# Two heads' compressed scores per product, the first norms inside the compression, and the first causal parts in front of the meeting

## The reference, cut to what matters

```python
h = _rmsnorm(x, norm1_g); proj = h @ w_in
q = _rmsnorm(proj[..., :o1].reshape(B, T, N_KV, HPG, HEAD_DIM), q_norm_g)   # 16 heads of 64, 4 groups
kv = proj[..., o1:o2].reshape(B, T, 6, N_KV, HEAD_DIM)
k_cmp = _rmsnorm(_compress(kv[:, :, 0], ...), k_norm_g[0])   # 31 blocks of 32 tokens; einsum, gelu, einsum
v_cmp = _compress(kv[:, :, 1], ...)
k_slc = _rmsnorm(kv[:, :, 2], k_norm_g[1]); k_win = _rmsnorm(kv[:, :, 4], k_norm_g[2])
s = jnp.einsum('bqghd,bngd->bghqn', qb, k_cmp) * scale
p_cmp = _masked_softmax(s - slopes * dist, dist >= 0)
o_cmp = jnp.einsum('bghqn,bngd->bqghd', p_cmp, v_cmp)
o = gb[..., 0:1] * o_cmp + gb[..., 1:2] * o_slc + gb[..., 2:3] * o_win
```

## Time and profile before

| | us |
|---|---|
| median of three runs | 3345.44 |
| the profiled execution's own time | 3342.76 |
| its span | 3341.0 |
| PE busy | 3247.5 (97% of the span) |
| DVE busy | 1785.4 (53%) |
| ACT busy | 1297.1 (39%) |
| mean granted TensorE clock | 0.978 |

### The profile page before, as it was taken

One profiled execution on the slowest core, in us unless ns is written; L12 is line 12 of the kernel. 1 busy time (PEld: TensorE's weight loads), 2 busy tenths in 40 slices (PEclk: granted clock), 3 DMA queues, 4 the chain that ended last, 5 costly groups with the idle time before them and its releaser, 6 DMA issues.

```text
span 3341.0 us, 41312 instructions
## 1 busy us (share of the span) xinstructions
PE 3247.5 (97%) x15343; PEld 2620.3 (78%) x15343; DVE 1785.4 (53%) x2671; ACT 1297.1 (39%) x1849; POOL 205.7 (6%) x230
## 2 busy tenths in 40 slices
PE   8989998999999999999999999999999999999998
PEld 6668976888888888876688888888888668888887
DVE  7357696445553455335765555345553566555532
ACT  4227755233332333323266333333322325633332
POOL 1001100000000000010110000010000011010000
PEclk9959999999999999999999999999999999999999
DMA  5320033333333333332312333333333322233332
GB/s 127 87 67 1 2 82 87 94 94 94 98 96 93 95 94 99 93 106 70 76 30 69 99 91 97 92 98 93 97 93 96 84 58 53 64 95 94 94 93 65
DMA packets 518489, 276.53 MB, mean 83 GB/s; under 512 B 39499, under 2 KB 510383, under 8 KB 518226
## 3 DMA queue, kind: packets, MB, share of 16 engines
q1 hardware_dynamic: 513154, 262.77, 28.6%
q0 software_dynamic: 3840, 11.26, 1.4%
q10 hardware_dynamic: 1360, 0.66, 0.1%
HBM read 264.11 MB, written 2.14 MB: 80 GB/s over the span
## 4 chain that ended last, share of the span: by engine, by line
PE 89%; DVE 7%; ACT 2%; issue 1%; DVEq 0%; DMA 0%; POOL 0%; ACTq 0%; POOLq 0%
PE bank L375 25%; PE bank L377 24%; PE bank L376 24%; PE bank L968 5%; PE bank L949 4%; PE bank L957 3%; PE bank L2386 1%; DVE wlo L351 1%; PE bank L1685 1%; PE bank L2359 1%; PE bank L2371 0%; DVE xc L1891 0%; DVE std L2571 0%; PE bank L687 0%; PE bank L1704 0%
## 5 line engine op out<-in xcount | busy, mean ns | idle before, releaser
L375 PE MATMUL bank<-hhi,whi 128*128 128x512 f32 (+1 forms) x2504 | 991.9, 396 | 7.5 <-DVE wlo L351 5.1
L377 PE MATMUL bank<-hlo,whi 128*128 128x512 f32 (+1 forms) x2504 | 977.0, 390 | 0.0
L376 PE MATMUL bank<-hhi,wlo 128*128 128x512 f32 (+1 forms) x2504 | 976.7, 390 | 0.0
L351 DVE TENSOR_TENSOR wlo<-raw,whi 128x1024 fp32r<-128x1024 f32 x485 | 608.9, 1258 | 585.0 <-ACT whi L344 576.2
L344 ACT CAST whi<-raw 128x1024 fp32r<-128x1024 f32 x485 | 505.1, 1046 | 408.6 <-PE bank L377 395.0
L375 PEld LDWEIGHTS bank<-hhi,whi 128*128 128x128 f32 (+1 forms) x2504 | 470.6, 188 | 147.3 <-issue 43.5
L376 PEld LDWEIGHTS bank<-hhi,wlo 128*128 128x128 f32 (+1 forms) x2504 | 470.7, 188 | 99.6 <-issue 3.4
L377 PEld LDWEIGHTS bank<-hlo,whi 128*128 128x128 f32 (+1 forms) x2504 | 470.1, 188 | 100.3
L375 PE MATMUL bank<-uhi,whi 128*128 128x512 f32 x880 | 348.6, 396 | 0.0
L376 PE MATMUL bank<-uhi,wlo 128*128 128x512 f32 x880 | 348.0, 395 | 0.0
L377 PE MATMUL bank<-ulo,whi 128*128 128x512 f32 x880 | 348.0, 395 | 0.0
(11 more groups left out here) (444 smaller groups left out, 3623.7 us busy)
## 6 DMA issues: line engine op xcount, KB each, us to landing
raw<-in_ffn_w_gate SPq DMA_DIRECT2D x88, 512.0 KB, 4.0
raw<-in_ffn_w_up SPq DMA_DIRECT2D x88, 512.0 KB, 3.8
raw<-in_w_in SPq DMA_DIRECT2D x78, 512.0 KB, 3.8
raw<-in_ffn_w_down SPq DMA_DIRECT2D x64, 512.0 KB, 4.1
raw<-in_w_out SPq DMA_DIRECT2D x24, 512.0 KB, 4.2
raw<-in_ffn_w_down SPq DMA_DIRECT2D x32, 384.0 KB, 3.5
raw<-in_w_gate SPq DMA_DIRECT2D x22, 512.0 KB, 4.1
raw<-in_w_up SPq DMA_DIRECT2D x22, 512.0 KB, 3.8
```

Source lines behind the costliest of these rows:

```text
L351: k.nc.vector.tensor_tensor(k.wlo[:, slot, :], k.raw[:, slot, :], k.whi[:, slot, :].bitcast(F32), ALU.subtract)\
L375: mm(out, whi, hi(kc), start=start and i == 0, stop=False)
L376: mm(out, wlo, hi(kc), start=False, stop=False)
L377: last = mm(out, whi, lo(kc), start=False, stop=stop and i == kcs - 1)
```

## The change

The score products of the compressed attention take two groups' keys as 64 moving columns for the same left operand, so a tile has 8 products in place of 16; each writes two pieces of 32 columns. `first_norms` and its meeting go; the 12 items, keys first, run inside `compress`: PE's spreads in pairs at five places, DVE's multiplications in pairs at five places and the last four behind the second gelu. The tables' loads wait for `hid_done` of b = 1, as their tiles and `q` now lie where the inputs of the compression were. The parts for group 0 and heads 0 and 1 are made by DVE at the end of `compressed_attention`, ahead of its meeting, and the meeting at the start of `causal_attention` goes. `normalize` (not shown again) is removed.

```diff
@@ -768,7 +768,7 @@
 def spread_scale(k, item, i, back, parts, heads):
-    k.nc.tensor.matmul(k.bank[5 - i % 2][0:item["rows"], :], back[0:2 * heads, item["norm"], 0:item["rows"]],
+    k.nc.tensor.matmul(k.bank[7 - i % 2][0:item["rows"], :], back[0:2 * heads, item["norm"], 0:item["rows"]],
                        parts[0:2 * heads, :], start=True, stop=True).then_inc(*k.spread_done.up())
...
@@ -1319,27 +1235,23 @@
                         first_projection(k, mem, otok, kT, vals, gates, dhi, dlo, back, scales)
                         store_tables(k)
                         handover(k)
-                    with ExitStack() as mem:
-                        compress(k, w, mem, dhi, dlo, kcmp, vcmp, gates)
-                        handover(k)
-                q, dist = sb("q", [P, KC, T], F32, q_mem), sb("dist", [P, T], F32, q_mem)
+                q = sb("q", [P, KC, T], F32, q_mem)
+                dist = sb("dist", [P, T], F32, q_mem)
                 cmp_mem = ExitStack()
                 bias, mask = sb("cmpbias", [P, TB, NH * 32], F32, cmp_mem), sb("cmpmask", [P, TB, 32], F32, cmp_mem)
-                @k.block.gpsimd
-                def _(pool):
-                    pool.dma_start(bias[:, :, :], k.consts["cmpbias"]).then_inc(*k.stage_landed.up(by=16))
-                    pool.dma_start(mask[:, :, :], k.consts["cmpmask"]).then_inc(*k.stage_landed.up(by=16))
-                    pool.dma_start(dist[:, :], k.consts["dist"]).then_inc(*k.stage_landed.up(by=16))
-                first_norms(k, otok, q, kT, back, scales)
-                handover(k)
+                with ExitStack() as mem:
+                    sb("dups", [P, 16 * T - (KC * T + T + TB * NH * 32 + TB * 32)], F32, mem)
+                    compress(k, w, mem, dhi, dlo, kcmp, vcmp, gates, first_items(k, otok, q, kT), back, scales[1],
+                             ((bias[:, :, :], "cmpbias"), (mask[:, :, :], "cmpmask"), (dist[:, :], "dist")))
+                    handover(k)
+            stacked = sb("qparts", [P, 2, T], F32R, q_mem, "right")
+            keys = sb("kparts", [P, 2, 2, 2, T], F32R, q_mem, "right")
             with cmp_mem as mem:
                 compressed_attention(k, mem, q, kcmp, vcmp, gates, otok, bias, mask)
+                first_parts(k, q, kT, stacked, keys)
                 handover(k)
             with ExitStack() as mem:
-                causal_attention(k, mem, q, dist, kT, vals, gates, otok)
+                causal_attention(k, mem, q, dist, kT, vals, gates, otok, stacked, keys)
                 outputs = k.pt_copied.all(), k.o_read.all(), k.o_added.all()
                 handover(k, pe_waits=False)
             q_mem.close()
@@ -1408,32 +1320,51 @@
     head_scales(k, *scales, NORM1_HEADS)
-def first_norms(k, otok, q, kT, back, scales):
-    nc = k.nc
-    gain = k.std[:, 0:1]
+def first_items(k, otok, q, kT):
+    items = [dict(norm=KC + c, rows=P, src=kT[:, c, :], out=kT[:, c, :],
+                  gain=vector(k, "k_norm_g", 1 + c // 2)[:, 0:1]) for c in range(4)]
+    return items + [dict(norm=c, rows=P, src=raw_queries(otok, c), out=q[:, c, :], gain=k.std[:, 0:1])
+                    for c in range(KC)]
+def head_parts(k, dve, q, stacked, h):
+    rows, c = query_rows(h)
+    k.nc.vector.tensor_copy(stacked[rows, h % 2, :], q[rows, c, :]).then_inc(*k.q_high.up())
+    dve.wait_ge(*k.q_high.all())
+    k.nc.vector.tensor_tensor(stacked[HD - rows.start:P - rows.start, h % 2, :], q[rows, c, :],
+                              stacked[rows, h % 2, :].bitcast(F32), ALU.subtract).then_inc(*k.q_parts.up())
+def key_parts(k, dve, kT, keys, g, b):
+    rows, _ = query_rows(HPG * g)
+    halves = (rows, slice(HD - rows.start, P - rows.start))
+    src, hi, lo = kT[rows, 2 * b + g // 2, :], keys[:, g % 2, b, 0, :], keys[:, g % 2, b, 1, :]
+    for to in halves:
+        last = k.nc.vector.tensor_copy(hi[to], src)
+    last.then_inc(*k.k_high.up())
+    dve.wait_ge(*k.k_high.all())
+    for to in halves:
+        last = k.nc.vector.tensor_tensor(lo[to], src, hi[rows].bitcast(F32), ALU.subtract)
+    last.then_inc(*k.k_parts.up())
+def first_parts(k, q, kT, stacked, keys):
     @k.block.vector
     def _(dve):
-        nc.vector.tensor_scalar(gain, vector(k, "q_norm_g")[:, 0:1], -HD ** -0.5, None, ALU.mult)\
-            .then_inc(*k.small_ready.up())
-        dve.wait_ge(*k.small_ready.all())
-    items = [dict(norm=c, rows=P, src=raw_queries(otok, c), out=q[:, c, :], gain=gain) for c in range(KC)]
-    items += [dict(norm=KC + c, rows=P, src=kT[:, c, :], out=kT[:, c, :],
-                   gain=vector(k, "k_norm_g", 1 + c // 2)[:, 0:1]) for c in range(4)]
-    normalize(k, items, back, scales[1], NORM1_HEADS)
-def causal_attention(k, mem, q, dist, kT, vals, gates, otok):
+        for b in range(2):
+            key_parts(k, dve, kT, keys, 0, b)
+            head_parts(k, dve, q, stacked, b)
+def causal_attention(k, mem, q, dist, kT, vals, gates, otok, stacked, keys):
     nc = k.nc
     sb = lambda name, shape, dt=F32: mem.enter_context(nc.sbuf_tensor(k.name(name), shape, dt))
     bias = sb("bias", [P, 2, T])
-    stacked, keys = sb("qparts", [P, 2, T], F32R), sb("kparts", [P, 2, 2, 2, T], F32R)
-    handover(k)
     groups, builds = [], []
     for h in range(NH):
         g = h // HPG
@@ -1447,40 +1378,24 @@
                             values=[vals[b][:, i, g, :] for i in range(t + 1)]) for t in range(TB)],
                 out=otok[:, :, h * HD:(h + 1) * HD], add=True, factor=gates[:, :, 3 * h + 1 + b]))
-    other = lambda rows: slice(HD - rows.start, P - rows.start)
-    head_at = {8 * h: h + 1 for h in range(NH - 1)}
-    head_at[-1] = 0
+    head_at = {8 * h: h + 1 for h in range(1, NH - 1)}
     keys_at = {32 * g + 3 + 8 * b: (g + 1, b) for g in range(NG - 1) for b in range(2)}
-    keys_at.update({-1: (0, 0), 0: (0, 1)})
     order = [keys_at[t] for t in sorted(keys_at)]
-    ready = {8 * h: [k.q_parts.at(h + 1)] for h in range(NH)}
-    for g in range(NG):
+    ready = {8 * h: [k.q_parts.at(h - 1)] for h in range(2, NH)}
+    for g in range(1, NG):
         for b in range(2):
             ready.setdefault(32 * g + 4 * b, []).append(k.k_parts.at(order.index((g, b)) + 1))
     def both_parts(dve, t):
         if t in keys_at:
             g, b = keys_at[t]
-            rows, _ = query_rows(HPG * g)
-            src, hi, lo = kT[rows, 2 * b + g // 2, :], keys[:, g % 2, b, 0, :], keys[:, g % 2, b, 1, :]
             if g >= 2:
                 dve.wait_ge(*k.qk_done.at(32 * (g - 1)))
-            for to in (rows, other(rows)):
-                last = nc.vector.tensor_copy(hi[to], src)
-            last.then_inc(*k.k_high.up())
-            dve.wait_ge(*k.k_high.at(order.index((g, b)) + 1))
-            for to in (rows, other(rows)):
-                last = nc.vector.tensor_tensor(lo[to], src, hi[rows].bitcast(F32), ALU.subtract)
-            last.then_inc(*k.k_parts.up())
+            key_parts(k, dve, kT, keys, g, b)
         if t in head_at:
             h = head_at[t]
-            rows, c = query_rows(h)
-            if h >= 2:
-                dve.wait_ge(*k.qk_done.at(8 * (h - 1)))
-            nc.vector.tensor_copy(stacked[rows, h % 2, :], q[rows, c, :]).then_inc(*k.q_high.up())
-            dve.wait_ge(*k.q_high.at(h + 1))
-            nc.vector.tensor_tensor(stacked[other(rows), h % 2, :], q[rows, c, :], stacked[rows, h % 2, :].bitcast(F32),
-                                    ALU.subtract).then_inc(*k.q_parts.up())
+            dve.wait_ge(*k.qk_done.at(8 * (h - 1)))
+            head_parts(k, dve, q, stacked, h)
     attention(k, groups, mem, builds, ready=ready, splits=both_parts)
...
@@ -1529,8 +1444,7 @@
     return bass.AP(ap.tensor, ap.offset, dims)
...
@@ -1542,6 +1456,7 @@
     w2k, w2v, b2v, b1 = sb("w2k", [P, 2, P]), sb("w2v", [P, 2, HD]), sb("b2v", [1, HD]), sb("b1", [1, 2, CMP_H])
     kraw, ksq, kroot = sb("kraw", [P, cols]), sb("ksq", [P, cols]), sb("kroot", [P, cols])
     n0 = k.unit
+    scales_ready = k.rn_ready.all()
     @k.block.gpsimd
     def _(pool):
@@ -1558,11 +1473,26 @@
         pool.memset(vcmp[:, :, :], 0.0).then_inc(*k.cmp_zero.up())
     loaded = k.stage_landed.all()
+    @k.block.gpsimd
+    def _(pool):
+        pool.wait_ge(*k.hid_done.at(2))
+        for tile, name in tables:
+            pool.dma_start(tile, k.consts[name]).then_inc(*k.stage_landed.up(by=16))
     on_act, on_act_tanh, on_dve, on_dve_end = gelu_steps(
         k, lambda b: z[b][0:cols, :], lambda b: hid[b][0:cols, :], k.gelu_act, k.gelu_dve, lambda b: k.z_ready.at(b + 1))
     @k.block.tensor
     def _(pe):
+        def spread(*which):
+            for i in which:
+                if i == 0:
+                    pe.wait_ge(*scales_ready)
+                if i >= 2:
+                    pe.wait_ge(*k.xn_done.at(i - 1))
+                spread_scale(k, items[i], i, back, parts, NORM1_HEADS)
         def turn(b):
             pe.wait_ge(*k.hid_ready.at(b + 1))
             for f in range(2):
@@ -1584,23 +1514,27 @@
```

(32 more changed lines are left out.)

73 lines of the change are left out of this document (removed).

## The result

The changed kernel takes 3325.73 us (median of four runs, 3324.43 to 3329.01) against 3344.64 us of the kernel before, run beside it: a ratio of 0.9941 with a 95% interval of 0.9927 to 0.9955, some 19 us faster (15 to 24). The forecast was 11.85 us faster, 3333.6; the measured median lies 0.2 us inside the lower end of its range (3325.5). The profiled execution is the slowest of the four: 3329.01 us, with a span of 3327.2.

The account below looks back on a forecast made before the run. PE was taken as the bound, busy for 97% of the span. Terms +1.0 - 6.65 - 6.2 = -11.85 us gave 3333.6 us on the median, range 3325.5 to 3339.5 to hold 8 in 10.

Parts of the forecast that it names:

- First edit: Norms moved inside the compression: their 10.8 us come back as waits, scores begin 1.0 us later than before.
- Steps 2 to 5: Compression queues: PE stands before spread 2, b = 1 ends at 184.1, DVE stands at norm 4, last spreads at 197.6.
- Second edit: Score products of the compressed attention at 64 columns: 6.65 us gained from first score to last copy.
- I take 0.26, the row of the same form: Price of one 64-column score product at 1.2 GHz, 0.26 us, taken from L1605's four products in 1.04 us.
- I take the new ones at 1.2 GHz: Last tile's scores: 16 products at 0.26 take 4.16 us where 3.65 was at full clock, 0.5 us lost.
- Third edit: Parts made ahead of the meeting and one meeting less at the causal stage's start: 6.2 us gained.
- the two prices that I stood between: Step 4's bias in the causal stage: 6.9 us earlier by DVE's work alone, 5.5 by PE; 6.2 was taken.
- The cover of the parts: End of compressed attention: 8.1 us between DVE's last work and ACT's last copy hide 7.0 of parts, 1.1 to spare.
- the clock rises in the scores, or columns are free: Rival for the score products: 2 to 4 us more gained, near 3330; chance 12%.
- The norms do hide: Rival for the compression: b = 1 and the stage end 2 to 5 us sooner, 3326 to 3331; chance 15%.
- cost goes by columns: Rival for the score products: 0.431 us each, 3 us lost in place of 6.65 gained, 3343; chance 10%.
- Slower: Rival: causal stage starts into a low clock and stays there; gain gone after 24 us more, 3363 at 60; chance 3%.

Follow-up runs that it names:

- the two repeats: The changed kernel run again twice with no edit, against the kernel before: ratios 0.9936 and 0.9945, medians 3325.02 and 3326.95 us.

## Why the prediction was right or wrong

**First edit: right in mechanism, 1 us short.** Steps 2 to 5 hold, each stand at its place: 3.66 us at spread 2 (forecast 3.7), 5.98 at norm 4 (about 5.2). To the first score it is 2.1 us more than before where I had 1.0; the norms' pairs run in the same 1.63 us. Part of the excess is chance: the clock came back at between 4.3 and 6.0 us behind the last scale part in the five profiles, and in the two repeats, where it did so at about the same point (5.4), the difference is 1.5. That the placing cost the time is shown by the runs with moved spreads: 4.9 us come back by moving spreads 2 and 3 alone, 8.7 by moving all.

**Second edit: the term that failed.** I had it at 6.65 us; it brought 12.2 in the changed kernel and 12.3 alone. Two steps were wrong.

The smaller one is "I take 0.26, the row of the same form": 1.25 us. L1605's 1.04 us run from the first of four instructions to the first of another kind. In the trace the four start 0.27, 0.22 and 0.21 us apart, and the instruction with a single row behind them 0.35 later; I read a gap between two lines as a pace. The pace is in the score products themselves, 0.213 us for 32, 64 and 128 columns. The row at hand hinted at it: 0.2155 us are 258 cycles of 1.2 GHz for 32 columns, many more than the columns. And the Trainium skill (TensorE: Matmul & The Clock Gate, "Back-to-back issue gap") has 1 to 64 columns on one floor. I quoted it, worked out 2.1 us and set it aside. The trace agrees in that 32 and 64 columns cost the same, but the floor here is some 256 cycles at 1.2 GHz, not about 60, and holds up to 128 columns. The first turn came 8.4 us sooner (forecast 7.15).

The larger one is the clock behind the first turn: "I take the new ones at 1.2 GHz" for the last tile's scores, and "behind that, turns and copies run as before". That was 0.5 us lost by forecast; from the first turn to the last copy it took 22.3 us in the first profile where it was 26.0, 3.7 gained, so 4.2 us are missing here. In all three profiles of the changed kernel the last tile's scores ran at full clock (2.06 to 2.15 us, forecast 4.16), and the values of two or three of the three later tiles took 1.99 us instead of 3.7. That these 3.7 us come with the columns is shown from both sides: alone they give 3.9 behind the first turn, and undoing them puts the last copy back to 46.0. But which products are the fast ones changes from kernel to kernel. The last tile's scores ran at 1.2 GHz with the columns alone, with the norms apart and with the moved spreads (2 of 2), at 2.4 GHz in the changed kernel (3 of 3) and with the parts undone, and at both with spreads 2 and 3 later. Why, stays open; that the clock came up early in both kernels with 128 columns is shown, by one profile each.

**Third edit: right in the changed kernel, and in part by the clock's luck.** 7.3 us by the first profile and 7.1 by undoing it, 6.2 forecast; of the two prices that I stood between, DVE's 6.9 was the nearer. PE's clock was up again at 240.7 and stayed, so steps 0 to 4 took 4.08 us; with the clock down they took 5.17. The cover of the parts, 1.1 us by forecast, was 0.8 in the first profile and 1.45 too little when the values were fast. Where the last tile's scores ran at 1.2 GHz and the last two tiles' values at full clock, the cover was 2.3 us too little and the edit brought 3.9 us. With both at 1.2 GHz, as I had assumed, no run shows it.

**Sum.** +2.1 - 19.4 for the two later lengths together = -17.3 by the profiles, where I had +1.0 - 12.85. Of the 5.4 us between them, by the first profile, 1.25 come from the price of a product, 4.2 from the clock behind the first turn, 1.1 from the third edit, and the first edit takes 1.1 back. The rival "the clock rises in the scores, or columns are free" had the mechanism, with 12% and at 3330, 2 to 4 us more: columns were free, the clock rose in the last tile's scores, though not in the first ones, and the second edit was worth 5.5 us more. "The norms do hide" and "cost goes by columns" fell by the runs. "Slower" fell: with the parts in front the clock was up again at most 5.8 us behind the first step's bias in every profile.

## What to carry to other kernels

A pace is read from a long run of one instruction (20.69 us for 96), never from the distance between two lines of different kinds. Where small products are at their floor, widen them: up to 128 columns it cost nothing here, and with 128 the clock came up sooner in both kernels that had them. Work moved into a stage's gaps hides only if each queue meets it where the other has already delivered: write down for both queues what stands ahead of every handed-over item, since here the items cost in the compression all of the 10.8 us of their old stage and 2.1 more, and placing them anew gave 8.7 back. And work hidden behind another engine's last step is hidden only as long as that step isn't sooner done: the same edit brought 7.1 us or 3.9.

## What was not expected of the hardware

- Score instructions in fp32, each with a left operand of 128 columns, start 0.213 us apart at 1.2 GHz and 0.112 at 2.4 GHz, with 32, 64 and 128 moving columns alike.
- 20.7 us of unbroken 32-column products and 10.5 of 64-column ones left the clock at 1.2 GHz; with 128 columns it rose 4.0 us behind the first (one profile).
- Two executions of one kernel differ by 11 us through the clock of one untouched stretch (0.74 against 0.94 over 60 us), while the sums of the edited stretch agree to 0.2 us in three.
